# Six reorderings on the tensor, scalar and vector queues of a three-block transformer kernel

## The reference, cut to what matters

```
def even_layer(x, ...):
    h = rms_norm(x, norm_mix) * (1 + sc_m) + sh_m
    fq, fk, fv, fgl, sq, sk, sv = split(h @ w_in)     # fgl: 8 outputs, the others 128 to 512
    log_f = log_sigmoid(fgl + forget_b)
    o_fox = forgetting_attention(fq, fk, fv, log_f)   # 8 heads of 64
    o_swa = sliding_window_sink_attention(rope(sq), rope(sk), sv, sinks)   # 8 heads
    x = x + g_m * (concat(o_fox, o_swa) @ w_out)
    return x + g_f * swiglu(rms_norm(x, ...), ...)

def odd_layer(x, ...):
    h = rms_norm(x, norm_mix) * (1 + sc_m) + sh_m
    q, k, v, iq, ik, iw = split(h @ w_in)             # iw: 8 outputs
    score = sum(iw[h] * relu(rope(iq)[h] @ rope(ik).T) for h in range(8))
    keep = the 64 largest of each row of score        # causal
    o = attention(rope(q), rope(k), v, keep)          # 16 heads of 64
    x = x + g_m * (o @ w_out)
    return x + g_f * moe_swiglu(rms_norm(x, ...), ...)   # 8 experts, 2 per token
```

## Time and profile before

| | |
|---|---|
| median of 3 runs | 1267.29 us (1265.4 to 1267.48) |
| the profiled execution, its own time | 1263.85 us |
| its span, first to last instruction | 1262.2 us |
| mean granted PE clock | 0.999 |
| PE busy | 1229.3 us (97%) |
| DVE, ACT, POOL busy | 671.6, 277.8, 88.5 us |

### The profile page before, as it was taken

The page is one execution under the profiler, slowest core; times in us unless marked ns, Lnnn a source line. Parts: engine busy times, 40 slices in busy tenths (PEclk is TensorE's granted clock), DMA queues, the critical chain, the costliest instruction groups (busy, mean ns, idle before and its releaser), DMA issues.

```text
span 1262.2 us, 26659 instructions
## 1 busy us (share of the span) xinstructions
PE 1229.3 (97%) x10620; PEld 936.9 (74%) x10620; DVE 671.6 (53%) x1672; ACT 277.8 (22%) x739; POOL 88.5 (7%) x157
## 2 busy tenths in 40 slices
PE   6999999999999999999999999999999999999997
PEld 4758888999999767789999997776654455455445
DVE  5455563888888735546776777883541011101104
ACT  4332203212111414540000004275300000000001
POOL 0100000000000000000000000100021100110120
PEclk9999999999999999999999999999999999999999
DMA  9999884577777583146777785795599999999993
GB/s 355 414 399 412 334 283 149 176 273 269 267 276 277 199 314 103 34 167 217 260 277 278 269 316 186 296 375 128 222 383 396 420 399 397 400 422 399 397 399 151
DMA packets 74822, 368.78 MB, mean 292 GB/s; under 512 B 8740, under 2 KB 8996, under 8 KB 49979
## 3 DMA queue, kind: packets, MB, share of 16 engines
q1 hardware_dynamic: 56594, 271.22, 57.3%
q0 software_dynamic: 18160, 96.64, 20.2%
HBM read 347.76 MB, written 20.06 MB: 291 GB/s over the span
## 4 chain that ended last, share of the span: by engine, by line
PE 92%; DVE 3%; DMA 2%; ACT 1%; SPq 1%; issue 1%; DVEq 0%
PE banks L957 21%; PE banks L697 16%; PE banks L1283 13%; PE banks L944 12%; PE banks L1332 9%; PE banks L1307 5%; PE banks L722 4%; PE banks L826 2%; PE banks L786 2%; PE banks L1024 2%; PE banks L881 1%; DMA side<-ada 1%; PE banks L865 1%; DMA ring<-stream 1%; PE banks L894 1%; DVE side L1728 1%
## 5 line engine op out<-in xcount | busy, mean ns | idle before, releaser
L1728 DVE CUSTOM_DVE_ANT_0 side<-side 128x1024 f32<-128x1024 f32 x128 | 151.1, 1220 | 32.6 <-DMA side<-ada 32.5
L1283 PE MATMUL banks<-ring,arena 128*32 128x512 f32 x1536 | 166.3, 592 | 1.6 <-DVE arena L2244 1.6
L944 PE MATMUL banks<-arena,ring 128*128 128x256 f32 x704 | 158.6, 379 | 0.0
L944 PEld LDWEIGHTS banks<-arena,ring 128*128 128x128 f32 x704 | 130.7, 190 | 16.1
L697 PE MATMUL banks<-h,ring 128*128 128x256 f32 x640 | 141.8, 380 | 0.3
L1283 PEld LDWEIGHTS banks<-ring,arena 128*32 128x32 f32 x1536 | 51.5, 110 | 111.4 <-issue 110.2
L697 PEld LDWEIGHTS banks<-h,ring 128*128 128x128 f32 x640 | 120.4, 190 | 18.4 <-issue 2.2
L2347 DVE TENSOR_TENSOR arena<-arena,banks 128x256 f32<-128x256 f32 (+1 forms) x48 | 15.2, 330 | 179.0 <-ACT arena L1665 178.9
L697 PE MATMUL banks<-arena,ring 128*128 128x256 f32 x384 | 84.3, 380 | 0.7 <-ACT arena L1464 0.5
L957 PEld LDWEIGHTS banks<-h,ring 128*128 128x128 f32 x672 | 81.4, 192 | 2.2
L614 POOL DMA_DIRECT2D side<-ada x64 | 34.0, 532 | 687.7 <-DVE msum L1728 678.2
(11 more groups left out here) (332 smaller groups left out, 1553.3 us busy)
## 6 DMA issues: line engine op xcount, KB each, us to landing
ring<-stream SPq DMA_DIRECT2D x247, 512.0 KB, 5.5
ring<-experts SPq DMA_DIRECT2D x96, 1024.0 KB, 18.9
side<-ada POOLq DMA_DIRECT2D x64, 1024.0 KB, 7.6
side<-experts SPq DMA_DIRECT2D x24, 1024.0 KB, 20.5
arena<-experts SPq DMA_DIRECT2D x8, 1024.0 KB, 21.9
yrows<-side POOLq DMA_DIRECT2D x1, 6144.0 KB, 42.7
hrows<-side POOLq DMA_DIRECT2D x1, 5632.0 KB, 23.4
arena<-lasts SPq DMA_DIRECT2D x8, 512.0 KB, 22.2
```

Of the source, the lines that this page charges most:

```text
L944: last = pe.matmul(banks[:, 4 + c // 2, (c % 2) * T:(c % 2 + 1) * T], ring[:, s, c * P:(c + 1) * P], hid[:, j % 2, :], start=first and c % ...
L1283: ins = pe.matmul(banks[BLOCK * j:BLOCK * (j + 1), t, :], hg[:, t, k, :], ring[:, m, (j % 2) * 512:(j % 2 + 1) * 512], start=(k == 0), sto ...
L1728: dve.tensor_tensor_reduce(weights, weights, cond[:, 0 if layer0 else 1, :], 1.0, 0.0, ALU.mult, ALU.add, accum_out=msum[:, n:n + 1]).then ...
```

## The change

Six edits. None adds or removes a matmul; one moves the source of a copy.

1. `raw_units`: two products of the second unit go ahead of the norm sum.
2. `few_outputs` (`fgl`, `iw`) and `few_per_token` each go behind one more unit; the unit that is now first waits for the normalized chunks one by one. The plan of banks and ACT's order follow.
3. Even attention: PE no longer waits for the last two copies of `fv` ahead of the first scores, but ahead of the first values.
4. `attend`, steps 7 to 9 of the even and odd layer: `early_out` goes ahead of the transposes, and the last one is cut in two halves, with the values of pair 7 between them. (The first block's attention had this order already.)
5. `take_query`: the copy of the unit first, and the four rotated copies read that copy, not the bank. ACT waits for its own copy; DVE's wait for it falls away.
6. First expert pass: `rows_turned` ahead of the copy L2367.

```diff
 def raw_units(r, first, second):
     for k in range(KC - 2):
         raw_block(a.bank, a.pos, r, k)
+    for k in range(2):
+        raw_block(b.bank, b.pos, r, k)
     begin(U["stat", r])
     norm_sum(r)
     for k in range(KC - 2, KC):
         raw_block(a.bank, a.pos, r, k)
-    for k in range(2):
+    for k in range(2, 4):
         raw_block(b.bank, b.pos, r, k)
     norm_spread(r)
-    for k in range(2, KC):
+    for k in range(4, KC):
         raw_block(b.bank, b.pos, r, k)
...
             raw_units(2, ("fq", 0), ("fq", 1))
+            one(("fq", 2), r=2)
             few_outputs("fgl", 2)
-            one(("fq", 2))
+            one(("fq", 3))
             few_per_token("fgl")
-            one(("fq", 3))
...
-            for name in ("fk", 3), ("fk", 2), "cum", ("fv", 0), ("fv", 1):
+            for name in ("fk", 3), ("fk", 2), "cum":
                 pe.wait_ge(*taken(U[name]))
...
 def values(pair):
+    if pair[0].kind == "fox" and pair[0].i == 0:
+        pe.wait_ge(*taken(U["fv", 0]))
+        pe.wait_ge(*taken(U["fv", 1]))
...
 def attend(heads, between):
-    first = heads is first_heads
-    if 1 <= m <= len(pairs) and not first:
+    steps = between.get(2 * m, []) + between.get(2 * m + 1, [])
+    ahead = heads is first_heads or m + 1 >= len(pairs)
+    if 1 <= m <= len(pairs) and not ahead:
         transposes(pairs[m - 1][0])
-    for step in between.get(2 * m, []) + between.get(2 * m + 1, []):
+    for step in steps[:1] if m > len(pairs) else steps:
         step()
-    if 1 <= m <= len(pairs) and first:
+    if 1 <= m <= len(pairs) and ahead:
         transposes(pairs[m - 1][0])
     if m >= 2:
         values(pairs[m - 2])
+    for step in steps[1:] if m > len(pairs) else []:
+        step()
...
-            for k in range(7):
+            for k in range(6):
                 m = max(5, 3 + k)
                 between[2 * m] = between.get(2 * m, []) + [early_out("eo", oT2, 4, k)]
+            between[18] = [early_out("eo", oT2, 4, 6, columns) for columns in ((0, 1), (2, 3))]
...
 def take_query(c):
-    act.wait_ge(*u.done)
+    take(u, dqT[:, c, :], 0, T)
+    act.wait_ge(*taken(u))
     act.wait_ge(s_rope, 10 + c)
     for j in range(4):
-        act.activation(ropet[to, c % 3, :], banks[at, u.bank, 0:T], ACT.Copy, scale=1.0 if j % 2 else -1.0).then_inc(s_shift, 1)
-    take(u, dqT[:, c, :], 0, T)
+        act.activation(ropet[to, c % 3, :], dqT[at, c, :], ACT.Copy, scale=1.0 if j % 2 else -1.0).then_inc(s_shift, 1)
...
+                rows_turned(p)
                 if first:
                     dve.wait_ge(s_picktr, 2)
                     dve.tensor_copy(pickT[:, :, P:T], ...)
-                rows_turned(p)
```

More of the change, by code:

```diff
@@ L1194, in _ @@
             between = {2 * (c - 4): [dq(c)] for c in range(4, 8)}
-            for k in range(7):
+            for k in range(6):
                 m = max(4, 3 + k)
                 between[2 * m] = between.get(2 * m, []) + [early_out("oo", dqT, 12, k)]
+            between[18] = [early_out("oo", dqT, 12, 6, columns) for columns in ((0, 1), (2, 3))]
             attend(odd_heads, between)
```

27 lines of the change are left out of this document (13 added, 14 removed).

## The result

The changed kernel takes 1256.2 us (median of 4 runs, 1253.71 to 1257.08), beside 1266.89 us for the kernel before on the same chip: a ratio of 0.9914, with a 95% interval of 0.9896 to 0.9932. That is 10.7 us less. Predicted were 9.7 less and 1257.6, from the median of 1267.29 that was known then.

What follows compares the result with a forecast made beforehand. PE, busy 97% of the span, was taken to bound the kernel, so only its waits could be won: 2.5 + 0.9 + 1.2 + 1.0 + 1.3 + 1.2 + 1.6 = 9.7 us off the median 1267.29 gives 1257.6, range 1253.0 to 1262.0.

Steps and rivals of the forecast that it cites:

- Into the even layer: Edits 1 and 2: PE's hole before the norm sum filled, eight-output products no longer paced by ACT; 2.5 us won.
- The rival that edit 2 does nothing: Eight-output products cost 2.7 us even when fed; even layer wins 0.9, odd 0.4; 1259.8 us; chance 0.06.
- First scores: Edit 3, even layer: PE's wait for ACT's copy of `fv` goes; 0.9 us won, 0.5 at the least.
- Ends: Edit 4, ends of both attentions: waits of 1.85 us filled with output chunks, less a new wait; 1.2 us won per layer.
- The new wait at step 8: Ends of attentions: a chunk waits for pair 5's output, copied behind the last head's exponentials; 0.5 us plus 0.1 for signals.
- The rival that ACT and DVE hold what PE lets go: Attention ends win 0.3 us each, the start of the odd attention nothing; 6.9 us in all, 1260.4; chance 0.22.
- Into the odd layer: Edits 1 and 2 make PE 1.5 us early, edit 5 costs 0.5; DVE and the attention go on 1.0 earlier.
- DVE, busy ahead of its index sums, is not moved: Odd layer: DVE's first sum stays put, so PE's product 4 can be early by 1.5 us, not 2.5.
- Query copy first: Edit 5, odd attention: rotated copies come 0.45 to 0.5 us later; the bank is freed sooner, winning 1.3.
- The slower rival: Rotated copies out of the arena take 0.77 us or more instead of 0.39; at 0.8, 1270.6 us; chance 0.02.
- Rows turned first: Edit 6, first expert pass: DVE turns the next rows some 10 us ahead; PE's wait of 1.6 us goes.
- The rival that transfers hold the experts: Expert passes: next rows or weights land late, so edit 6 wins 0; 8.1 us in all, 1259.2; chance 0.10.

Runs made afterwards that it cites:

- e3: The changed kernel with edits 1 and 2 undone: 1260.18 us, ratio 0.9945 to the kernel before.
- e1: The changed kernel run again with no edit, five runs: 1255.78 us, ratio 0.9910 to the kernel before.
- e5: The changed kernel with edit 3 undone, PE again awaiting the value copies before the first even scores: 1255.43 us, ratio 0.9915 to the kernel before.
- e4: The changed kernel with edit 4 undone, transposes again ahead of output chunks in steps 7 to 9: 1257.79 us, ratio 0.9929 to the kernel before.
- e8: The changed kernel with ACT copying pair 5's output ahead of the last head's exponentials in step 7: 1253.37 us, ratio 0.9898 to the kernel before.
- e2: The changed kernel with edit 5 undone, rotated copies first and out of the bank: 1256.22 us, ratio 0.9917 to the kernel before.
- e6: The changed kernel with edit 6 undone, DVE's copy of turned picks again ahead of turning rows: 1257.09 us, ratio 0.9924 to the kernel before.
- e7: The changed kernel with edits 1 and 2 undone and GpSimd's zeroing put earlier: 1258.54 us, ratio 0.9943 to the kernel before.
- e10: The changed kernel with e8's edit and the load of the final gains issued behind the first expert pass: 1254.49 us, ratio 0.9909 to the kernel before.
- e11: The changed kernel with e8's output copy, later gains load, earlier zeroing and PE's two holes filled with unread products: 1252.72 us, ratio 0.9889 to the kernel before.

## Why the prediction was right, and where it was not

**Into the even layer: 2.5 predicted, 2.38 measured** (e3 against e1). The step was right in mechanism: 0.9 of hole and 1.66 of eight-output products, which were ACT's pace and not PE's own time. Their sum is 2.57; where the other 0.2 went was not followed. The rival that edit 2 does nothing falls.

**First scores: 0.9 predicted, 0.95 measured** (e5). The copy's place behind a table load on ACT cost nothing.

**Ends: 1.2 in each layer predicted, 1.11 and 1.30 to 1.37 measured** (e4). The new wait at step 8, put at 0.5 with 0.1 for signals, is 0.62 and 0.44, and e8 shows that it is the output copy behind exponentials, as worked out. The rival that ACT and DVE hold what PE lets go would have given 0.3 in each layer.

**Into the odd layer: 1.0 predicted, 1.29 to 1.53 measured, 1.8 to 2.0 without edit 5's share.** The step that failed is that DVE, busy ahead of its index sums, is not moved. It did begin its two first sums where it had before, 35.3 us behind the residual add, but they got shorter: before they took 1.32 us, until 0.2 behind the end of GpSimd's zeroing. With the change the zeroing comes 0.6 sooner behind the residual add, and the sums take 0.69; the relu that PE's product 4 needs starts 36.1 instead of 36.7 behind the residual add. That the 0.6 is the difference between 1.5 and 2.0 is worked out from these rows; no run moved the zeroing back in the changed kernel. Why it comes sooner: the transfer that it follows landed after 1.41 us of idle GpSimd with edits 1 and 2, and after 1.96 and 2.03 without; what moved that landing is open.

**Query copy first: 0.45 to 0.5 later predicted, 0.48 to 0.72 measured; the bank 1.3 predicted, 1.47 measured** (e2). A rotated copy out of the arena costs 0.43 instead of 0.39: 0.16 for four, which the prediction put at next to nothing. The 0.40 that it took for a copy from arena to arena is another instruction, the squaring of the residual (L1393, `h<-x`); it came near all the same. The slower rival needed 0.77 for one. The four follow one another end to end, 1.73 for four, as the row of before had it, and not with the overlap that the Trainium skill gives for back-to-back activations (ScalarE: Activation LUTs, section What ACT_TABLE_LOAD costs). Other activations of this kernel do overlap: the eight of L1416 take 0.59 each and start 0.49 apart.

**Rows turned first: 1.6 predicted, 1.7 measured** (e6). But the cover was thinner than said: the rows landed 11.7 us after their issue (930.49 to 942.17), so the turn came 2.5 us ahead of the last transposes (1.7 in e1), where the prediction had some 10 us. The rival that transfers hold the experts falls: no pass from the second to the last waited (300.0 in all profiles).

In five of the twelve profiles with edit 6 the first pass took 44.1 to 45.4 instead of 43.9, with pauses marked "issue" of 0.3 to 0.6 where the trace lists them. They are not waits for weights. In e8, with the longest, all 17 loads for this pass had landed 2.7 us before it began, and the matmul that starts behind the 0.61 in the first profile, at 939.63, has no semaphore wait and reads a weight chunk that PE was already using. What goes with the pauses is the loading of instructions. The page lists a DMA queue "q8 instruction" that brings 16 KB at a time; its second such transfer within the first pass began 23.3 to 24.0 us behind the pass's start in these five profiles, and 19.4 to 22.7 in the nine others, before and e6 included. No run moved these transfers by themselves, so that they are the cause is not shown.

**Sum: 9.7 predicted, 10.3 by stretches, 10.7 and 11.25 by medians.** The terms erred by little and mostly the same way. What the prediction left out of its sum is a change of TensorE's clock, which it named only as a sign of being wrong; the last section shows it in the changed kernel, where it cost 1.64 us in both profiles. That the medians came out as near to the sum as they did is luck in part: by their mean clocks the runs of both kernels hold such losses, of unequal size, and the sum has no term for them.

## What to carry to other kernels

Products paced by another engine's chunks look busy in the trace: four of the same kind with ready inputs took 0.64, which makes some 1.1 for the eight that showed as 2.73, and putting a full unit ahead of them was worth nearly the whole difference. A wait that a reordering leaves behind is worth reading to its last queue: at step 8 it was one copy behind exponentials, and moving it (e8) closed it. When a term looks bounded by an engine that is "busy", look at whether each of its instructions takes its usual time; a wait with the reason "issue" is not yet a wait for data: look at what has landed, and at the instruction queue; and short holes of PE ahead of long products may be worth filling, even with products that nobody reads.

## What the hardware showed that was not expected

**TensorE's clock fell behind two short holes.** The products that pick the rows, in the changed kernel and in the one before, and the windows of the changed kernel around them (columns as above):

```profile
894.28 5.41 PE L1253 MATMUL banks<-arena 128*128 128x96 f32 x32 [0.45 <-DVE arena L2215]
```

```profile
902.26 3.78 PE L1243 MATMUL banks<-arena 128*128 128x96 f32 x32 [0.45 <-DVE arena L2206]
```

```profile
892.00:894.00 2.00, 1.74 (x14) 1.53 (x14) 1.10 (x6) 1.99 (x5) 0.00 (x0) 1.00 0.96 397
894.00:896.00 2.00, 1.72 (x12) 1.75 (x13) 1.83 (x7) 0.46 (x1) 0.00 (x0) 0.79 0.29 115
896.00:898.00 2.00, 2.00 (x11) 2.00 (x11) 1.01 (x5) 0.00 (x0) 0.00 (x0) 0.50 0.00 0
898.00:900.00 2.00, 2.00 (x17) 1.89 (x16) 0.90 (x5) 0.00 (x0) 0.00 (x0) 0.86 0.00 0
```

Ahead of the fall PE stood 0.51 and 0.45 us, with ten matmuls of 128x8 and four of transposes between; then, from 0.5 to 1.1 us into the products, the granted clock was 0.50, 1.2 GHz in place of 2.4, for some 3.4 us, and the products took 1.63 us more. Of ten profiles of the changed kernel and its variants with these holes open, five show the fall (the change twice, e3, e5, e6) and five do not (e2, e4, e7, e8, e10); the holes are the same in all. Of three with the holes filled none shows it, and their twelve runs have a mean clock of 0.998 or 0.999, where six of the change's nine have 0.996 or 0.997. So the runs speak for a fall that comes and goes from one execution to the next, and for the holes being needed for it. Neither is settled. The only kernel profiled twice, the change, fell both times. The mean clock does not tell a single fall: e6's profiled run has 0.998 with the fall, and e8's four runs have 0.998 or 0.999 with the holes open. And the added products move more than the clock: with them the first pass's first 16 KB of instructions come 3.3 to 3.8 us behind its start instead of 7.2 to 7.7, and none of the three first passes paused, so the 3 us of the medians need not be the clock's alone.

Runs of the kernel before speak for such losses there too: its profile has a mean clock of 0.999 and no fall, but of the 36 runs beside the experiments five have 0.999 and take 1264.5 us in the mean, and fourteen have 0.995 or 0.996 and take 1268.1. That fits the profile of before lying 3.4 us below its median. And since the two profiles of the change each have a fall and it has none, they differ from it by only 6.9 and 8.1; medians are the ones to compare. Where the clock fell in those runs of before, no profile shows.

**GpSimd's zeroing held up two DVE operations.** The two TENSOR_SCALAR sums of 128x128 and 128x256, with one tensor input, took 1.24 us beside a zeroing by GpSimd (e3), ending 0.2 behind it, and 0.54 without (e7). The Trainium skill, SBUF — State Buffer, section Who interferes with whom, says that VectorE and GpSimd share one pair of ports and that it is an exclusive lock. The runs agree for these two. Other DVE operations were not held up: in the change a TENSOR_TENSOR and a TENSOR_REDUCE beside the same zeroing (797.01 to 797.53) took 0.22 and 0.27, as they did in e7 without it. In e11 the two sums took 0.79 beside a transfer issue of GpSimd; since the second sum stood beside such an issue in e7 and took its usual 0.35, that the issue held them up is not shown.
